# Parameter loads and later weight pieces issued once x's first half is turned: two waits moved in the SP queue of a three-layer transformer kernel

## The chip, the cores and the metric

One core of a Trainium2 chip runs the whole program. Its engines are TensorE (PE; PEld is its weight load), VectorE (DVE), ScalarE (ACT), GpSimd (POOL) and SyncE (SP), which here only issues DMA transfers. The metric is the device time of one execution in microseconds (us), and the kernel before is told by the median of three runs.

## The reference, cut to what matters

```
x = first_block(x, ...)          # mixer with GLA and dilated attention, then 32 experts, top 2
x = second_block(x, ...)         # two layers:
for i in range(2):
    hn = rms_norm(h, g_mix[i]);  z = hn @ w_in[i]            # in_0, in_1
    h = h + concat(gating(z_a), rwkv7(z_b), nsa(z_c)) @ w_out[i]
    hn = rms_norm(h, g_ffn[i])
    f = swiglu(hn, ...) if i == 0 else moe_swiglu(hn, ...)   # dense, then 8 experts, top 2
    h = h + f
    gate = sigmoid(rms_norm(h, g_ple[i]) @ ple_gate_w[i])    # ple_g
    h = h + (p[i] @ ple_proj_w[i]) * gate                    # ple_p
return rms_norm(h, g_final)
```

256 tokens, 1024 features, everything in float32. Inside `rwkv7` each row of z is mixed with the row before it, `z = z_b + (z_prev - z_b) * mu`.

## The kernel before, in words

**Order of the work.** Each engine has one hand-written list of instructions, and semaphores tie them. The stages are: the first block's mixer, the first expert stage (`moe1`), `in_0`; then in one stage the mixer of layer 0, its output projection, the dense layer, `ple_p0`, `ple_g0` and `in_1`; then the mixer of layer 1, the second expert stage (`moe2`), and last `ple_p1`, `ple_g1` and the final norm.

**The stream of weights.** All weights come in pieces of 1 MB (128 partitions by 2048 floats, 1.05 MB), in the order of their use, into a ring of nine slots (`RAW = 9`). The SP queue issues them: `stream` waits, for piece n, until TensorE has used piece n - 9, which had the same slot (`sp.wait_ge(used, p.n - RAW + 1)`), and then issues the transfer. SP works strictly in order, so whatever it waits for holds everything behind.

**Splitting.** A product runs as three matmuls on an upper and a lower part. ScalarE casts a landed piece into its upper part (L586, `split_high`), VectorE subtracts that to get the lower part in place (L590, `split_low`), TensorE then uses the piece (L566 to L568, 24 matmuls). `split_until` sends both ahead of TensorE by a few pieces, at places written out by hand in each engine's list; a piece that hasn't landed holds ScalarE there, with all that stands behind.

**Turning x.** Before a product with x, TensorE transposes x in two halves of four chunks each (`turn_half`, L667, eight transposes a half). Every chunk counts up the semaphore `xT_psum`. ScalarE evacuates the upper part with the norm's gain (L689), VectorE the lower part (L693). `XT_AT[name]` is the count before the transposes of one product, so `XT_AT[name] + KC // 2`, that is plus 4, is its first half turned.

**The expert stages' end.** TensorE scatters the last results (L2109, L2110) and VectorE adds them to x (L2294). Then each engine tests whether an expert has more tokens than fit (`overfull`) and, where none has, jumps over the code of an overflow pass (`stage_moe_rest`). Behind the jump stand, for ScalarE and VectorE, the splits of the next one or two pieces, and for TensorE the transposes of x.

**The SP queue around `in_0`.** `in_0` has twelve pieces. SP issued 0 to 5, waited until the last expert piece was used, and issued the 20 parameter loads of layer 0 (`load_layer`, L816: rows, small matrices and two transposed position tables), then pieces 6 to 9. Behind them stand four copies within SBUF that shift z by one row (`shift_sp`, L2511 to L2515, once ScalarE has evacuated the second job), which VectorE's mix (L2523 to L2525) waits for together with the parameter loads. ScalarE's two sigmoids (L2600, L2601) follow on that mix, and TensorE's small products of L2553 and L2559 on those.

**The SP queue around `ple_g`.** After the last piece of the feed-forward part come one piece of `ple_p` and four of `ple_g` (two blocks of 512 columns, each in two halves of the contraction), then, in layer 0, the pieces of `in_1`. In `ple_part(0)` ScalarE casts `ple_g0`'s piece 1 between the upper parts of x's two halves, with two result copies (L3503) behind it; pieces 2 and 3 follow after the squares of the norm (L710). In `ple_part(1)` all transposes come first, and pieces 1 to 3 are cast from the norm on.

Of the kernel before, what the change touches and what calls it, by code (L numbers as in the profile page):

```python
# [31 lines left out]
KC = D // P  # L32
# [85 lines left out]
def emit(nc, d, out):  # L118
    ctx = ExitStack()
    with ctx:  # L120
# [5 lines left out]
        def sem(name):  # L126
            return ctx.enter_context(nc.semaphore(name))
# [79 lines left out]
        upper, split, used = sem("upper"), sem("split"), sem("used")  # L207
# [49 lines left out]
        def sig(name):  # L257

            name = step_place[name][0] if name in step_place else name
            if name not in sems:  # L260
                sems[name] = sem(name)
            return sems[name]

        def ended(name, k=1, layer=0, per_layer=0):

            if name in step_place:
                _, before, total = step_place[name]
                return sig(name), layer * total + before + k
            return sig(name), layer * per_layer + k
# [4 lines left out]
        jobs_of, pieces_of = {}, {}  # L274
# [23 lines left out]
        def project(name, weight, kc, width, engines, group, first=0, striped=False, blocks=None, banks=(0, 1, 2, 3), k_first=False):  # L298
# [46 lines left out]
            for k, part in enumerate(parts):  # L345
                n = sum(m for _, m in part)
                places = [sum(m for _, m in part[:i]) for i in range(len(part))]
                chunks = kc if kc * n <= PIECE else kc // 2
                for c in range(0, kc, chunks):
                    p = new_piece([(0, chunks * n, rows[:, c:c + chunks, c0:c0 + m], n, at) for (c0, m), at in zip(part, places)], group)  # L350
                    p.c0, p.chunks, p.width, p.last = c, chunks, n, c + chunks == kc
                    pieces_of[name].append(p)
                    if c == 0:
                        jobs(p, k if blocks else part[0][0], n, 0)
                    else:
                        p.jobs = pieces_of[name][-2].jobs
                    if p.last:
                        done(p)
# [89 lines left out]
        moe1 = plan_moe("moe1", d["w_gate"][0], d["w_up"][0], d["w_down"][0], N_GROUPS, PER_GROUP, DE1, d["norm2_g"])  # L448
# [39 lines left out]
        def stream(sp, pieces):  # L488
            for p in pieces:
                if p.n >= RAW:  # L490
                    sp.wait_ge(used, p.n - RAW + 1)
                for dst, src in p.copies:
                    sp.dma_start(dst, src).then_inc(piece_ready[p.slot], 16)
# [34 lines left out]
        def stream_moe(sp, f):  # L528
            lot = [p for st in f.plan for p in st.up] + [p for st in f.plan for p in st.down]
            stream(sp, sorted(lot, key=lambda p: p.n))  # L530
            sp.wait_ge(sig("counted"), f.number)
            with overfull(sp, f):
                sp.wait_ge(used, f.until)
                m2 = Pass()
                stream_bucket(sp, f, m2, 0)
                with sp.Fori(1, f.buckets) as g:
                    stream_bucket(sp, f, m2, g)
                sp.wait_ge(*m2.at("used", f.buckets * f.steps))
            sp.end_ifs()
            if f is moe1:  # L540
                sp.sem_inc(sig("rest_streamed"), 1)
# [186 lines left out]
        XT_AT = {name: KC * k for k, name in enumerate(XT_ORDER)}  # L728
# [85 lines left out]
        def load_layer(eng, l):  # L814
            for dst, src in layer_loads(l):
                eng.dma_start(dst, src).then_inc(sig("layer_params"), 16)  # L816
# [1686 lines left out]
        def shift_sp(sp, l, part):  # L2503

            cols = (slice(512, 1024), slice(0, 512))[part]
            done = sig(f"rw_prev{part}")
            sp.wait_ge(evac_act, max(j.evac for j in jobs_of[f"in_{l}"][2 * part:2 * part + 2]))
            zb = z[:, :, ZB0:ZC0][:, :, cols]
            prev = w_prev[:, :, cols]
            even = P - 16  # L2510
            sp.dma_start(prev[1:even + 1], zb[0:even]).then_inc(done, 16)  # L2511
            for t in range(NT):
                sp.dma_start(prev[even + 1:P, t, :].rearrange("p (a n) -> p a n", a=16),
                             zb[even:P - 1, t, :].rearrange("p (a n) -> p a n", a=16)).then_inc(done, 16)
            sp.dma_start(prev[0:1, 1, :].rearrange("p (a n) -> p a n", a=16),  # L2515
                         zb[P - 1:P, 0, :].rearrange("p (a n) -> p a n", a=16)).then_inc(done, 16)
# [1133 lines left out]
        @block.sync  # L3650
        def _(sp):

            sp.dma_start(x[:], d["x"][0].rearrange("(t p) n -> p t n", p=P)).then_inc(sig("x_ready"), 16)
            sp.dma_start(g1T[:], d["norm1_g"][0].rearrange("(p c) -> p c", c=KC)).then_inc(sig("x_ready"), 16)
            stream(sp, pieces_of["in_ab"][0:3])
            for dst, src in G_LOADS:
                sp.dma_start(dst, src).then_inc(sig("g_params"), 16)
            stream(sp, pieces_of["in_ab"][3:7])
            for dst, src in P1_LOADS:
                sp.dma_start(dst, src).then_inc(sig("params"), 16)  # L3660
            stream(sp, pieces_of["in_ab"][7:])
            for name in ("gates", "y_gla", "y_att", "out_1"):
                stream(sp, pieces_of[name])
            stream_moe(sp, moe1)
            for l in range(LAYERS):
                pieces = pieces_of[f"in_{l}"]
                if l == 0:
                    stream(sp, pieces[0:6])
                    sp.wait_ge(used, moe1.until)
                    load_layer(sp, 0)  # L3670
                    stream(sp, pieces[6:10])
                else:
                    stream(sp, pieces[0:10])
                shift_sp(sp, l, 0)
                stream(sp, pieces[10:])
                shift_sp(sp, l, 1)
                stream(sp, cmp_pieces[l])
                stream(sp, pieces_of[f"out_{l}_2"])
                if l == 0:
                    sp.wait_ge(*ended("nsa_cmp", 1))  # L3680
                    load_layer(sp, 1)
                    stream(sp, sorted([p for up in ffn.up for p in up] + ffn.down, key=lambda p: p.n))
                else:
                    stream_moe(sp, moe2)
                stream(sp, pieces_of[f"ple_p{l}"])
                stream(sp, pieces_of[f"ple_g{l}"])

        @block.tensor
        def _(pe):
# [41 lines left out]
```

## Time and profile before

| | |
|---|---|
| median of 3 runs | 2472.41 us (2471.65 to 2475.49) |
| profiled execution | 2472.59 us, span 2470.8 us, mean granted TensorE clock 0.971 |
| PE busy | 2319.1 us (94%) |
| DVE busy | 1842.4 us (75%) |
| ACT busy | 1467.2 us (59%) |
| DMA | 617.64 MB, 250 GB/s over the span |

All times in the rows are from the start of the span. The profiled execution's own time is 1.8 us longer than its span. In the timeline a row is one instruction, or several alike in a row (x4), with the time from the start of the first to the end of the last; in square brackets stands how long the engine was idle ahead of it and what ended that. "issue" there means that nothing which the profile shows was waited for. SPq rows are DMA issues by the SP queue. In the rows of DMA queues q1 carries the SP queue's transfers, q8 and q14 carry instructions to the engines.

### The profile page before, as it was taken

How to read it: one execution, taken by the hardware profiler on the slowest of the kernel's cores; microseconds unless marked ns; L12 is line 12 of the kernel's file. 1: busy time of each engine (PE TensorE's matmuls, PEld its weight loads, DVE VectorE, ACT ScalarE, POOL GpSimd, SP SyncE). 2: the span in 40 equal slices, each digit the busy share in tenths (PEclk: the TensorE clock that was granted, in tenths of full speed). 3: DMA queues.
4: the chain of work that ended last, by engine and by line, in shares of the span. 5: the costliest groups of instructions: out<-in, count | busy, mean ns of one | idle time of the engine just before them, and what ended most of it. 6: DMA issues, size and time to landing. Idle time of an engine off the chain costs nothing.

```text
span 2470.8 us, 30555 instructions
## 1 busy us (share of the span) xinstructions
PE 2319.1 (94%) x12418; PEld 1891.6 (77%) x12418; DVE 1842.4 (75%) x1894; ACT 1467.2 (59%) x1400; POOL 49.6 (2%) x47
## 2 busy tenths in 40 slices
PE   7999987999999997988999998879999999999996
PEld 6878766888888885776788777668888888888885
DVE  5885658888898985776554577578888978888884
ACT  5354536776777774534443553466776767767764
POOL 0000000000000000020000002000000000000000
PEclk9999998999999998999999999989999999999999
DMA  9444445999999997406464551249999989999990
GB/s 231 128 124 136 153 145 186 363 367 358 366 359 367 357 368 231 138 3 196 138 203 171 166 163 50 81 177 363 356 366 357 358 300 349 358 368 355 366 344 34
DMA packets 281227, 617.64 MB, mean 250 GB/s; under 512 B 31848, under 2 KB 130408, under 8 KB 243696
## 3 DMA queue, kind: packets, MB, share of 16 engines
q1 hardware_dynamic: 279664, 611.33, 71.4%
q10 hardware_dynamic: 1408, 4.19, 0.5%
q8 instruction: 103, 1.69, 0.3%
q14 instruction: 52, 0.43, 0.1%
HBM read 612.34 MB, written 1.05 MB: 248 GB/s over the span
## 4 chain that ended last, share of the span: by engine, by line
PE 86%; DVE 7%; ACT 4%; issue 2%; POOL 0%; DMA 0%; DVEq 0%; ACTq 0%; SPq 0%
PE ps L566 25%; PE ps L567 25%; PE ps L568 25%; DVE ring_parts L590 2%; PE ps L2745 2%; PE ps L2098 1%; ACT high_parts L586 1%; PE ps L3023 1%; PE ps L667 1%; DVE arena L3280 0%; DVE arena L1325 0%; PE ps L3036 0%; PE ps L2068 0%; PE ps L2109 0%; PE ps L2110 0%
## 5 line engine op out<-in xcount | busy, mean ns | idle before, releaser
L590 DVE TENSOR_TENSOR ring_parts<-ring,high_parts 128x2048 fp32r<-128x2048 f32 (+1 forms) x574 | 1283.4, 2276 | 181.6 <-ACT high_parts L586 170.0
L586 ACT CAST high_parts<-ring 128x2048 fp32r<-128x2048 f32 (+1 forms) x574 | 1079.5, 1897 | 203.9 <-PE ps L568 190.6
L568 PE MATMUL ps<-high_parts,arena_parts 128*128 128x512 f32 (+2 forms) x1560 | 620.2, 398 | 0.0
L566 PE MATMUL ps<-high_parts,hT_parts 128*128 128x512 f32 (+2 forms) x1120 | 456.4, 408 | 30.5 <-DVE ring_parts L590 12.6
L567 PE MATMUL ps<-ring_parts,hT_parts 128*128 128x512 f32 (+2 forms) x1120 | 445.3, 398 | 0.0
L566 PE MATMUL ps<-high_parts 128*128 128x512 f32 x912 | 365.2, 400 | 0.0
L567 PE MATMUL ps<-ring_parts,high_parts 128*128 128x512 f32 x912 | 359.3, 394 | 0.0
L568 PE MATMUL ps<-high_parts 128*128 128x512 f32 x912 | 356.5, 391 | 0.0
L568 PEld LDWEIGHTS ps<-high_parts,arena_parts 128*128 128x128 f32 x1560 | 299.5, 192 | 68.9
L566 PE MATMUL ps<-high_parts,arena_parts 128*128 128x512 f32 x744 | 293.8, 395 | 3.2 <-DVE arena_parts L2273 2.3
L567 PE MATMUL ps<-ring_parts,arena_parts 128*128 128x512 f32 x744 | 292.9, 394 | 0.0
L566 PEld LDWEIGHTS ps<-high_parts,hT_parts 128*128 128x128 f32 x1120 | 217.9, 195 | 85.5 <-issue 21.4
L567 PEld LDWEIGHTS ps<-ring_parts,hT_parts 128*128 128x128 f32 x1120 | 217.6, 194 | 47.3
L568 PEld LDWEIGHTS ps<-high_parts 128*128 128x128 f32 x912 | 171.4, 188 | 41.7
L566 PEld LDWEIGHTS ps<-high_parts 128*128 128x128 f32 x912 | 172.1, 189 | 37.8
L567 PEld LDWEIGHTS ps<-ring_parts,high_parts 128*128 128x128 f32 x912 | 171.0, 187 | 35.7
L566 PEld LDWEIGHTS ps<-high_parts,arena_parts 128*128 128x128 f32 x744 | 140.3, 189 | 36.3 <-DVE arena_parts L2273 2.7
L2288 DVE SCALAR_TENSOR_TENSOR arena<-ps,arena 128x512 f32<-128x512 f32 x80 | 57.9, 724 | 147.7 <-PE ps L568 132.4
L567 PEld LDWEIGHTS ps<-ring_parts,arena_parts 128*128 128x128 f32 x744 | 140.1, 188 | 32.2
L2202 ACT CAST arena_parts<-ps 128x512 fp32r<-128x512 f32 x80 | 45.4, 567 | 140.1 <-PE ps L2098 140.1
L568 PE MATMUL ps<-high_parts,hT_parts 128*128 128x512 f32 x304 | 120.0, 395 | 0.0
L2220 ACT ACTIVATE arena<-ps 128x512 f32<-128x512 f32 x80 | 46.2, 578 | 68.0 <-PE ps L568 68.0
(525 smaller groups left out, 1831.0 us busy)
## 6 DMA issues: line engine op xcount, KB each, us to landing
ring<-in_moe_w SPq DMA_DIRECT2D x248, 1024.0 KB, 5.4
ring<-in_w_gate SPq DMA_DIRECT2D x64, 1024.0 KB, 5.3
ring<-in_w_up SPq DMA_DIRECT2D x64, 1024.0 KB, 5.2
ring<-in_w_down SPq DMA_DIRECT2D x64, 1024.0 KB, 5.3
ring<-in_w_in SPq DMA_DIRECT2D x104, 256.0 KB, 4.5
ring<-in_ffn_w SPq DMA_DIRECT2D x44, 512.0 KB, 4.8
ring<-in_w_in SPq DMA_DIRECT2D x20, 1024.0 KB, 5.0
ring<-in_moe_w SPq DMA_DIRECT2D x32, 512.0 KB, 4.8
```

The costliest lines, as they stand in the source:

```text
L566: pe.matmul(dst, a_hi, b_hi, start=first, stop=False, skip_group_check=True)
L567: pe.matmul(dst, a_hi, b_lo, start=False, stop=False, skip_group_check=True)
L568: return pe.matmul(dst, a_lo, b_hi, start=False, stop=last, skip_group_check=True)
L586: act.copy(high_flat(p), raw_flat(p)).then_inc(upper, 1)
L590: dve.tensor_tensor(raw_flat(p, ring_parts_flat), raw_flat(p), f32(high_flat(p)), ALU.subtract).then_inc(split, 1)
L667: mm = pe.transpose(ps[:, banks[c % 4 // 2], (c % 2) * S + t * P:(c % 2) * S + (t + 1) * P], src[:, t, c * P:(c + 1) * P], ident[:])
L2098: mm = pe.transpose(ps[:, TURN, c * P:(c + 1) * P], m_hid[:, 0:st.n][:, c::nc_], ident[:])
L2202: act.copy(m_hidT[:, 0:st.n // P, :].rearrange("p c n -> p (c n)"), ps[:, TURN, 0:st.n])\
L2220: act.activation(m_sg[:, 0:st.n], ps[:, GATE, 0:st.n], ACT.Silu).then_inc(sig("moe_silu"), 1)
L2288: dve.scalar_tensor_tensor(out=m_hid[:, 0:st.n], in0=src, scalar=m_gate[:, q:q + 1], in1=m_sg[:, 0:st.n], op0=ALU.mult, op1=ALU.mult).then ...
L2745: mm = pe.matmul(ps[rows, bank, i * RC:(i + 1) * RC], a[rows, i, :], b[rows, i, :], start=True, stop=True)
L3023: mm = pe.matmul(ps[0:CG * NCMP, CHAIN, k * P:(k + 1) * P], n_blk[:, k, i, :], w[:, i, :], start=(i == 0), stop=(i == 15))
```

## The change

SP's list gets two new waits on `xT_psum` and loses one on `used`. In `in_0`, pieces 4 and 5, the parameter loads and everything behind them are issued once the first half of x is turned for `mix0`. In both layers, pieces 1 to 3 of `ple_g` and everything behind them are issued once the first half of x is turned for `ple0` or `ple1`.

```
             for l in range(LAYERS):
                 pieces = pieces_of[f"in_{l}"]
                 if l == 0:
-                    stream(sp, pieces[0:6])
-                    sp.wait_ge(used, moe1.until)
+                    stream(sp, pieces[0:4])
+                    sp.wait_ge(sig("xT_psum"), XT_AT["mix0"] + KC // 2)
+                    stream(sp, pieces[4:6])
                     load_layer(sp, 0)
                     stream(sp, pieces[6:10])
                 else:
...
                 stream(sp, pieces_of[f"ple_p{l}"])
-                stream(sp, pieces_of[f"ple_g{l}"])
+                stream(sp, pieces_of[f"ple_g{l}"][0:1])
+                sp.wait_ge(sig("xT_psum"), XT_AT[f"ple{l}"] + KC // 2)
+                stream(sp, pieces_of[f"ple_g{l}"][1:])
```

On the SP queue at the end of the first expert stage (`ring` is the ring of weight pieces, `in_w_in` the weights of `in_0`), before (-) and in the change (+):

```order
-L493 DMA ring<-in_w_in 128x4x512 [waits used] x6
-L816 DMA arena<-in_rw_mu 128x1024 [waits used]
+L493 DMA ring<-in_w_in 128x4x512 [waits used] x4
+L493 DMA ring<-in_w_in 128x4x512 [waits used,xT_psum]
+L493 DMA ring<-in_w_in 128x4x512 [waits used]
+L816 DMA arena<-in_rw_mu 128x1024
 L816 DMA arena<-in_rw_w_2 128x256
 L816 DMA arena<-in_rw_a_2 128x256
```

No transfer changes its place in the queue; the fifth piece gets the wait on `xT_psum`, and the first parameter load loses its own.

On the SP queue at the end of the dense layer, ahead of the pieces of `in_1`:

```order
 L493 DMA ring<-in_ple_proj_w 128x2x1024 [waits used]
-L493 DMA ring<-in_ple_gate_w 128x4x512 [waits used] x4
+L493 DMA ring<-in_ple_gate_w 128x4x512 [waits used]
+L493 DMA ring<-in_ple_gate_w 128x4x512 [waits used,xT_psum]
+L493 DMA ring<-in_ple_gate_w 128x4x512 [waits used] x2
 L493 DMA ring<-in_w_in 128x4x512 [waits used] x10
```

The second gate piece gets the wait, and the ten pieces of `in_1` stand behind it. The same happens at the end of the second expert stage, where nothing stands behind.

## Rows read from the trace of the kernel before

**Rows 1.** The page: the chain by engine, and one kind of DMA issue.

```profile
PE 86%; DVE 7%; ACT 4%; issue 2%; POOL 0%; DMA 0%; DVEq 0%; ACTq 0%; SPq 0%
...
ring<-in_w_in SPq DMA_DIRECT2D x20, 1024.0 KB, 5.0
```

**Rows 2.** Timeline, end of the first expert stage: start, duration, engine, what, idle before.

```profile
953.42 0.34 SPq L816 DMA_DIRECT2D arena<-in_rw_mu  x1
...
959.04 3.70 ACT L586 CAST high_parts<-ring 128x2048 fp32r<-128x2048 f32 x2 [4.61 <-issue]
...
967.17 1.97 PE L667 MATMUL ps<-ident,x 128*128 128x128 f32 x8 [8.47 <-issue]
968.01 2.29 DVE L590 TENSOR_TENSOR ring_parts<-ring,high_parts 128x2048 fp32r<-128x2048 f32 x1 [8.58 <-issue]
...
970.63 0.43 SPq L816 DMA_DIRECT2D arena<-in_nsa_vc_w  x1
...
971.97 0.76 PE L566 MATMUL ps<-high_parts,hT_parts 128*128 128x512 f32 x1 [2.83 <-issue]
```

**Rows 3.** DMA queues in two stretches, 964.2 to 964.4 and 2422.6 to 2422.8.

```profile
q8 instruction: 1, 0.02, 42.6%
...
q8 instruction: 2, 0.03, 118.6%
```

**Rows 4.** Windows: engines' busy time, then granted PE clock, DMA share, GB/s.

```profile
955.00:970.00 15.00, 4.92 (x16) 3.38 (x16) 5.35 (x6) 5.36 (x6) 0.00 (x0) 0.56 0.79 145
...
2417.00:2424.00 7.00, 2.31 (x8) 1.35 (x8) 4.24 (x6) 2.29 (x2) 0.00 (x0) 1.00 0.27 83
...
973.00:980.00 7.00, 7.00 (x28) 5.55 (x27) 1.19 (x4) 2.12 (x5) 0.00 (x0) 0.70 1.05 393
989.00:994.00 5.00, 5.00 (x23) 4.01 (x22) 2.38 (x2) 2.10 (x2) 0.00 (x0) 1.00 0.42 112
```

**Rows 5.** Timeline of the SP queue: pieces 0 to 5 and the first shift copy.

```profile
928.59 14.73 SPq L493 DMA_DIRECT2D ring<-in_w_in  x6
...
989.34 0.73 SPq L2511 DMA_DIRECT2D arena<-arena  x1
```

**Rows 6.** Timeline, end of the second expert stage and the cast of `ple_g1`'s piece 1.

```profile
2419.32 1.90 ACT L586 CAST high_parts<-ring 128x2048 fp32r<-128x2048 f32 x1 [1.92 <-issue]
...
2424.24 2.29 DVE L590 TENSOR_TENSOR ring_parts<-ring,high_parts 128x2048 fp32r<-128x2048 f32 x1 [2.77 <-issue]
...
2426.76 3.68 PE L667 MATMUL ps<-ident,x 128*128 128x128 f32 x16 [6.24 <-issue]
...
2428.86 3.43 DVE L693 SCALAR_TENSOR_TENSOR arena_parts<-ps,l_gT,hT_parts 128x256 fp32r<-128x256 f32 x8 [2.33 <-ACT hT_parts L689]
...
2439.21 1.89 ACT L586 CAST high_parts<-ring 128x2048 fp32r<-128x2048 f32 x1
```

**Rows 7.** Timeline of the SP queue: first and last of layer 1's 20 parameter loads.

```profile
1112.06 0.34 SPq L816 DMA_DIRECT2D arena<-in_rw_mu  x1
...
1127.03 0.43 SPq L816 DMA_DIRECT2D arena<-in_nsa_vc_w  x1
```

**Rows 8.** Timelines of DVE and PE in `in_0`: the mix, and TensorE's wait behind it.

```profile
998.42 0.69 DVE L2523 TENSOR_TENSOR arena<-arena 128x512 f32<-128x512 f32 x1
...
1008.19 0.48 PE L2559 MATMUL ps<-arena 64*128 64x256 f32 x1 [1.86 <-DVE arena L2651]
```

**Rows 9.** Timelines of PE and ACT in `ple_part(0)`.

```profile
1369.94 1.03 PE L667 MATMUL ps<-ident,x 128*128 128x128 f32 x8
...
1380.08 0.40 PE L566 MATMUL ps<-high_parts,hT_parts 128*128 128x512 f32 x1
...
1372.06 1.93 ACT L586 CAST high_parts<-ring 128x2048 fp32r<-128x2048 f32 x1
...
1374.80 1.62 ACT L689 ACTIVATE hT_parts<-ps,l_gT 128x256 fp32r<-128x256 f32 x4
...
1380.07 3.69 ACT L586 CAST high_parts<-ring 128x2048 fp32r<-128x2048 f32 x2
```

## The prediction

> **What bounds the kernel now.** I read the page first: TensorE carries 86% of the chain that ended last [rows 1]. So time counts only where it comes on TensorE's path, and I looked at the three places at which the change moves a wait of the SP queue: the ends of the two expert stages and the end of the dense layer. There I read the timeline, for the bracketed idle time ahead of a row.
>
> At the end of the first expert stage the first transpose of x starts at 967.17, behind 8.47 us of idle put down to "issue": TensorE had been done since 958.70, and VectorE, which stands 8.58 us itself, had added its last to x by 959.43 [rows 2]. ScalarE stands 4.61 us. All three have just jumped over the code of the overflow pass, and the instruction queue's rows show what TensorE waits for: a block of q8 lands at 964.2, 5.5 us after its last matmul and 2.9 us ahead of the restart [rows 3]. Meanwhile the 20 parameter loads pass, issued from 953.42 to 971.06 [rows 2], and the DMA engines are busy to 0.79 [rows 4]. Weight pieces 4 and 5 are not among them: the last of the six was issued by 943.3 [rows 5] and had landed when the loads began.
>
> The second expert stage ends in the same jump without such loads (share 0.27) [rows 4]. There ScalarE stands 1.92 us, VectorE 2.77, TensorE 6.24 [rows 6]; two q8 blocks land at 2422.6, 2.1 us after TensorE's last matmul ended at 2420.52 [rows 3]. By this pair I price the change.
>
> The Trainium skill ("Runtime: NRT & Kernel Launch", section "Instruction fetch mechanics") says that a taken branch to code outside the fetched pages stalls the engine until a DMA has brought the page; the trace agrees, with the q8 block 2.9 us ahead of the restart.
>
> **The change, part by part.** It adds no work; only SP's waits move. The wait that goes, on the last expert piece, is implied by the new one: nothing.
>
> *First expert stage, the gain.* The loads no longer pass during the jump. ScalarE resumes at 954.43 + 1.92 = 956.4 and VectorE at 959.43 + 2.77 = 962.2 [rows 2, 6]. TensorE: 958.70 + 2.1 to the landing + 2.9 or 4.1 (both stages' time from landing to restart) = 963.7 or 964.8. I take 963.7, the one measured at this very jump. If the landing takes no more than ScalarE's 1.92 us of standing, VectorE is the last, from 962.2. Today VectorE must first split piece 0 (968.01, 2.29 us), and the first product with x starts at 971.97, 4.8 us after the transposes [rows 2]. At the second stage the lower halves begin 2.1 us after the first transpose, and four take 1.7 us (eight 3.43) [rows 6]: with VectorE early, the product starts 3.9 us behind the transposes, at 967.6. **Gain there 4.4 us**, bounds 3.2 (restart 964.8) and 5.8 (VectorE's 962.2 + 2.29 + 1.7 = 966.2).
>
> *What is late next.* SP starts when four chunks are turned, 963.7 + 2.0 (eight transposes, 1.97) = 965.7, and not at 953.42. It issues pieces 4 and 5, the 20 loads, pieces 6 to 9, and then the four copies that shift z by a row. Two pieces: 0.9 us, at 0.43 an issue as its last load. The loads: 17.6 us here, 15.4 for layer 1 (1112.06 to 1127.46) [rows 7]; I take 16.5, between them. So pieces 6 to 9 start at 983.1. The first lands 5.0 us later [rows 1]; they are 1.05 MB each, at the 393 GB/s of 973 to 980 [rows 4] 2.67 us apart, so the last lands at 983.1 + 5.0 + 8.0 = 996.1. In the old order they were through long before the shift copies were issued at 989.34 [rows 5]. Now those, wanted at 985, stand behind them in SP's ring, and take 2.1 us of their own (0.42 of the 5 us from 989 to 994 [rows 4]): 998.2. VectorE's mix waits for them; it started at 998.42 right behind the split of piece 5 [rows 8], would be ready at 994.0 with the gain, and finds its input at 998.2. ScalarE's sigmoids, the casts behind them and VectorE's copies hang on it, and TensorE has no slack there, since it waits 1.86 us for those at 1008.19 [rows 8]: it gives the gain back. **Net -0.2 us**, bounds -4.4 (copies not held; -5.8 with the best jump) and +3 (a late restart with loads of 17.6 us). Piece 6 lands at 988 and is used after six pieces of 5.7 us, near 1002: nothing.
>
> *Dense layer's end (ple0).* No jump stands here, so there is nothing to gain. The gate weights lay in the ring long before. Now pieces 1 to 3 are issued when the transposes of 1369.94 are done, at 1371.0 [rows 9], and the first lands at 1376.0, 3.9 us after ScalarE began its cast (1372.06). ScalarE works in order, so two result copies and the second half of x (1374.80) wait too. New: cast to 1377.9, copies to 1378.8, second half to 1380.4; VectorE's subtraction 1378.0 to 1380.3, then its four lower halves to 1382.0. TensorE came to that piece at 1380.08 without waiting [rows 9], so it stands 1.9 us. From the second half of x to the next casts (1374.80 to 1380.07) ScalarE needs 5.3 us [rows 9]: casts from 1384.1, so piece 2 is cast by 1386.1 and subtracted by 1388.4. TensorE is ready at 1382.0 + 5.7 (1374.4 to 1380.08 is one piece) = 1387.7: another 0.8. The other pieces have landed by then. The next turn of x follows from these gates, so all of it stays. **Cost 2.7 us**, bounds 1.5 and 4 (a landing 1.2 us earlier or later).
>
> *Second expert stage (ple1).* The gate pieces had landed before the jump (share 0.27, most of it a gain vector's), so nothing is gained. Now they are issued at 2426.76 + 2.0 = 2428.8, land at 2433.8, 2436.5 and 2439.2, and the first is cast at 2439.21 [rows 6], the others more than 3 us later. Cost 0; the cover of 5.4 us would end with a landing over 10 us.
>
> **Sum:** -0.2 + 2.7 + 0 = +2.5 us. The profiled execution took 2472.59 around its span of 2470.8, 0.18 over the median of 2472.41: so 2475.1 against it, **2474.9** on the median.
>
> **Rivals.** (A) *The fetch doesn't depend on the loads.* TensorE restarts at 967.17 as before, SP starts at 969.1, the shift lands at 1001.6, and the mix with all behind it is 3.2 us late; with ple0 +5.9: 2478.3. From a restart later than 963.9 on, the first stage loses. For it: TensorE stood 6.24 us with hardly a load about. Against: all three engines stood longer under the loads, and q8 landed 3.4 us later.
 The landing at 964.2 speaks against it.
> (B) *The copies aren't held*, because the loads are issued faster or the ring lets them by: 4.4 stays, less 2.7: 2470.7. For it: the mix had to wait for nothing before.
> (C) *B, and ple0 loses nothing*, TensorE having enough ahead: -4.4 to -5.8, 2468.0 to 2466.6.
> That the change doesn't do what it says is excluded by the order: the waits stand where the diff puts them.
>
> **Chances.** Forecast 0.52 (2472.5 to 2477.5), A 0.23, B 0.17, C 0.08. The range takes in B, and A with 2 us on top: 2469.5 to 2480.5; C and a double loss stay out. A measurement can tell about 0.2%, 4.9 us, from no change. Slower by more: most of A and a tenth of the forecast, 0.25. Faster by more: most of C, 0.07. Within: 0.68.
>
> **What would show it.** Right: first transpose near 963.7 behind 5 us of "issue"; the loads' first row behind it; VectorE's mix idle for about 4 us on the shift copies and starting at its old time; TensorE idle for 2 and 1 us in ple0 on VectorE's splits; ple1 as it was. Wrong: "issue" still at 8 us (A); the mix near 994 (B); no new idle in ple0 (C).

## The result and the profile after

The change is slower: 2483.66 us (median of 6 runs, 2480.49 to 2488.56) against 2472.68 (6 runs, 2470.17 to 2475.49), a ratio of 1.0043 with a 95% interval of 1.0033 to 1.0053. Of the 11.0 us the forecast had 2.5, and the result lies outside its range. The profiled execution took 2483.69 us around a span of 2481.9, so 11.1 more span than before; what follows is counted in that span.

First the page after, the chain by engine and the landing of the 1 MB weight pieces.

```profile
PE 85%; DVE 7%; ACT 3%; issue 2%; SPq 1%; DMA 1%; POOL 0%; DVEq 0%; ACTq 0%
...
ring<-in_w_in SPq DMA_DIRECT2D x20, 1024.0 KB, 9.1
```

Against [rows 1] SP's queue and DMA have each come into the chain with a percent, and the same pieces land after 9.1 us instead of 5.0. The kernel now waits for transfers that were hidden.

The end of the first expert stage, timeline after, as [rows 2] show it before (start, duration, engine, what, idle before).

```profile
954.23 1.01 ACT L2209 CAST arena_parts<-ps 128x1024 fp32r<-128x1024 f32 x1 [6.63 <-PE ps L568]
...
957.47 3.70 ACT L586 CAST high_parts<-ring 128x2048 fp32r<-128x2048 f32 x2 [2.22 <-issue]
...
962.75 1.97 PE L667 MATMUL ps<-ident,x 128*128 128x128 f32 x8 [3.27 <-issue]
963.31 2.29 DVE L590 TENSOR_TENSOR ring_parts<-ring,high_parts 128x2048 fp32r<-128x2048 f32 x1 [3.11 <-issue]
...
967.28 0.76 PE L566 MATMUL ps<-high_parts,hT_parts 128*128 128x512 f32 x1 [2.56 <-issue]
```

The cast at L2209 is the last work that the change can't touch; it starts at 954.23, before it was 953.42, so 0.8 us of every later difference is between the two executions and not the change's. The idle under "issue" fell from 8.47 to 3.27 us on TensorE, from 8.58 to 3.11 on VectorE, from 4.61 to 2.22 on ScalarE, and the first product starts at 967.28 instead of 971.97: with the 0.8 us, a gain of 5.5 us.

Then the SP queue, timeline after (start, time to issue, queue, what).

```profile
964.75 0.92 SPq L493 DMA_DIRECT2D ring<-in_w_in  x2
965.71 0.50 SPq L816 DMA_DIRECT2D arena<-in_rw_mu  x1
...
985.38 0.43 SPq L816 DMA_DIRECT2D arena<-in_nsa_vc_w  x1
985.85 2.25 SPq L493 DMA_DIRECT2D ring<-in_w_in  x4
988.14 2.92 SPq L2511 DMA_DIRECT2D arena<-arena  x1
991.10 2.81 SPq L2513 DMA_DIRECT2D arena<-arena  x2
```

The 20 loads take from 965.71 to 985.81, 20.1 us; the four pieces and the shift copies follow. The next rows are issues between 985 and 996 with their median time to landing, after.

```profile
ring<-in_w_in SPq DMA_DIRECT2D x4, 1024.0 KB, 10.1
...
arena<-arena SPq DMA_DIRECT2D x1, 448.0 KB, 12.9
arena<-arena SPq DMA_DIRECT2D x2, 30.0 KB, 9.4
...
arena<-arena SPq DMA_DIRECT2D x1, 2.0 KB, 11.1
```

Before, the copies in the same stretch:

```profile
arena<-arena SPq DMA_DIRECT2D x1, 448.0 KB, 3.5
arena<-arena SPq DMA_DIRECT2D x2, 30.0 KB, 2.7
arena<-arena SPq DMA_DIRECT2D x1, 2.0 KB, 3.7
```

What waits for them, and TensorE behind it, after:

```profile
1005.17 0.69 DVE L2523 TENSOR_TENSOR arena<-arena 128x512 f32<-128x512 f32 x1 [11.92 <-DMA arena<-arena]
...
1009.61 1.11 PE L2553 MATMUL ps<-ident,arena 128*128 128x128 f32 x4 [12.29 <-ACT arena L2601]
```

The mix stands 11.92 us and starts 6.75 us later than in [rows 8], TensorE's L2553 comes 6.74 later and has 12.29 us of idle where it had 0.28 (it started at 1002.87 before). With the 0.8 us taken off, the stage has lost 5.9 us, although its first product came 5.5 us early.

The end of the dense layer (`ple_part(0)`), timeline after, and a window in it (busy time of PE, PEld, DVE, ACT, POOL, then granted clock, DMA share, GB/s).

```profile
1377.55 1.03 PE L667 MATMUL ps<-ident,x 128*128 128x128 f32 x8
...
1378.62 1.47 SPq L493 DMA_DIRECT2D ring<-in_ple_gate_w  x3
...
1383.89 1.91 ACT L586 CAST high_parts<-ring 128x2048 fp32r<-128x2048 f32 x1 [4.08 <-DMA ring<-in_ple_gate_w]
...
1386.65 1.58 ACT L689 ACTIVATE hT_parts<-ps,l_gT 128x256 fp32r<-128x256 f32 x4
1389.84 0.47 PE L566 MATMUL ps<-high_parts,hT_parts 128*128 128x512 f32 x1 [1.98 <-DVE arena_parts L693]
```

```profile
1390.00:1394.00 4.00, 4.00 (x12) 3.15 (x12) 0.55 (x3) 3.97 (x6) 0.00 (x0) 0.63 1.05 387
```

ScalarE waits 4.08 us for the gate piece, TensorE 1.98 behind VectorE. Right behind that idle the granted clock is 0.63 of full speed: for most of the stretch TensorE is on the lower of its two levels (1.2 and 2.4 GHz), where a matmul takes 0.63 us instead of 0.39; before the change the stretch 1378 to 1392 had 1.00:

```profile
1378.00:1392.00 14.00, 14.00 (x65) 11.34 (x64) 7.42 (x8) 8.47 (x10) 0.00 (x0) 1.00 0.47 153
```

From this turn of x to the next it takes 25.14 us (1377.55 to 1402.69) instead of 21.35 (1369.94 to 1391.29): 3.8 us lost, about half by waiting, half by the clock.

The second expert stage lost nothing: its transposes stand 6.64 us under "issue" (6.24 in [rows 6]), the three gate pieces are issued at 2439.96 and land after 7.7, and the casts run on without a DMA in their brackets. TensorE's L667 there comes 11.2 us later than before, the end of the span 11.1. **The tally:** 0.8 between the executions, 6.8 by the turn of `ple0` (5.9 at the mix and some 0.9 on the way there), 3.8 in `ple0`, nothing after, together 11.4, against 11.1 at the end.

### The profile page after: what moved, and what is told of

The parts are those of the page before. It is cut to its first block, busy times and chain, and to the rows that moved or that the text cites. A ratio compares the mean times of both kernels' runs of the same rounds, so it can differ in the third digit from the quotient of the medians.

```text
span 2481.9 us, 30558 instructions
## 1 busy us (share of the span) xinstructions
PE 2324.9 (94%) x12418; PEld 1894.2 (76%) x12418; DVE 1842.4 (74%) x1894; ACT 1467.1 (59%) x1400; POOL 49.6 (2%) x47
## 4 chain that ended last, share of the span: by engine, by line
PE 85%; DVE 7%; ACT 3%; issue 2%; SPq 1%; DMA 1%; POOL 0%; DVEq 0%; ACTq 0%
PE ps L566 25%; PE ps L567 24%; PE ps L568 24%; DVE ring_parts L590 2%; PE ps L2745 2%; PE ps L2098 1%; ACT high_parts L586 1%; SPq L816 1%; PE ps L667 1%; PE ps L3023 1%; PE ps L3036 0%; DVE arena L3280 0%; PE ps L2109 0%; DMA arena<-arena 0%; PE ps L2110 0%
```

## The experiments

**The two parts alone.** `e1_in0_only` has the first hunk of the change on the kernel before, `e2_ple_only` the second. 

> The change's wait in in_0 alone, ple_g as in the kernel before. Additive theory: the loss is two separate ones, about 6 to 7 us here (jump shortened by 5 us, mix of in_0 about 6 us late) and about 3.7 us in ple0. Then this run is +6.5 us on the kernel before (5.5 to 8), and TensorE shows no new idle in ple_part(0). Rival: the loss in ple0 is only there because the stage before is late; then this run shows the whole +11 us.

> The two waits on ple_g alone, in_0 as in the kernel before. Additive theory: +3.7 us (2.7 to 4.5), all of it in ple_part(0), where TensorE waits about 2 us for piece 1 and 1 to 2 us for piece 2; nothing in ple_part(1). Rival: +0 to 1 us, the loss coming only together with the other wait; or a loss in ple_part(1) too, then over +5 us.

Measured: e1 2479.78 us (6 runs) against 2474.37 (21 runs), ratio 1.0026 [1.0012, 1.0039]; e2 2477.24 (11 runs) against the same 21, ratio 1.0011 [1.0001, 1.0021]. The timeline of e1:

```profile
963.85 1.44 PE L667 MATMUL ps<-ident,x 128*128 128x128 f32 x8 [2.88 <-issue]
...
1005.09 0.69 DVE L2523 TENSOR_TENSOR arena<-arena 128x512 f32<-128x512 f32 x1 [9.47 <-DMA arena<-arena]
```

and of e2:

```profile
1381.98 1.91 ACT L586 CAST high_parts<-ring 128x2048 fp32r<-128x2048 f32 x1 [3.89 <-DMA ring<-in_ple_gate_w]
...
1387.92 0.47 PE L566 MATMUL ps<-high_parts,hT_parts 128*128 128x512 f32 x1 [1.79 <-DVE arena_parts L693]
```

The parts add up within their intervals: 0.26% and 0.11%, together 0.37%, beside the change's 0.43%. e1 has its forecast (+6.4 us by the ratio), e2's +2.7 is at the lower end of its own. In e1 the turn-to-turn time of `ple0` is 21.34 us, in e2 24.91, so each loss has its own part of the diff as its cause. From L2209 to the first turn of `ple0` it takes 422.54 us in e1, 423.32 in the change, 416.52 before; e9, which leaves `in_0` as before, has 416.56, but e2, which does so too, 417.83: up to 1.3 us of this distance differ from one execution to the next.

**Are the copies what is late?** `e3_copies_first` keeps every wait of the first hunk, but issues the four shift copies ahead of pieces 6 to 9:

```diff
                     load_layer(sp, 0)
+                    shift_sp(sp, l, 0)
                     stream(sp, pieces[6:10])
```

(the call that stood behind is left for layer 1 alone). `e4_nine_ahead` asks whether the whole can be had by order: pieces 0 to 8 before the wait, loads and piece 9 behind it.

```diff
-                    stream(sp, pieces[0:6])
-                    sp.wait_ge(used, moe1.until)
+                    stream(sp, pieces[0:9])
+                    sp.wait_ge(sig("xT_psum"), XT_AT["mix0"] + KC // 2)
                     load_layer(sp, 0)
-                    stream(sp, pieces[6:10])
+                    stream(sp, pieces[9:10])
```

> As the change in in_0 (ple_g as before), but the four shift copies are issued ahead of pieces 6 to 9. Theory 'ring': the mix is late because its copies stand behind 4 MB of weights in the ring. Then they land by 992 to 994, the mix starts near 994, TensorE's idle ahead of L2553 falls from 12.3 us to under 2, and the shorter jump is kept: -3 to -5 us on the kernel before. Rival 'late loads': the parameter loads (20 us of issue, begun 12 us later) are themselves what comes too late, or the copies are slow on their own; then the mix still starts at 1000 or later and the run is +2 us or more. A late piece 6 (issued near 989, cast near 997) may cost up to 2 us in either.

> Pieces 0 to 8 of in_0 are issued as soon as their slots are free, only the parameter loads and piece 9 wait for the first half of x; ple_g as before. Theory 'ring': the copies have one piece and the loads' tail ahead, land by 994, mix near 994, and the jump stays short: -3 to -5 us. If weights in large packets slow the instruction fetch as the small loads do, piece 8 and the tail of 7 (issued near 950 and 953) lengthen the jump to about 5 us or more of idle, and the gain is halved (-2 us). Rival 'late loads': mix at 1000 or later, +2 us or more.

Measured, against the same 21 runs: e3 2467.96 us (9 runs), ratio 0.9977 [0.9967, 0.9987]; e4 2467.20 (6 runs), ratio 0.9968 [0.9956, 0.9980]. Both beat both kernels, e3 by 5.7 us and e4 by 7.9 on the kernel before, somewhat more than the 3 to 5 forecast. e3's timeline:

```profile
963.79 1.44 PE L667 MATMUL ps<-ident,x 128*128 128x128 f32 x8 [2.76 <-issue]
...
995.55 0.69 DVE L2523 TENSOR_TENSOR arena<-arena 128x512 f32<-128x512 f32 x1
```

e4's:

```profile
965.47 0.34 SPq L816 DMA_DIRECT2D arena<-in_rw_mu  x1
...
993.60 0.69 DVE L2523 TENSOR_TENSOR arena<-arena 128x512 f32<-128x512 f32 x1
```

With the copies ahead of the pieces, the mix has no wait and starts 9.5 us before e1's; all else is the same. That settles the mechanism: the copies stood in SP's ring behind four 1 MB pieces. In e3 they land after 3.5, 2.7 and 3.4 us. The distance from L2209 to the turn of `ple0` is 412.24 us in e3 and 410.45 in e4, 4.3 and 6.1 under before: this is what the shorter jump is worth when nothing gives it back, to 1.3 us. e4's loads take 16.4 us to issue (965.47 to 981.89), e3's 19.85: with pieces 4 and 5 in the ring ahead of the loads, the issue of the loads is 3.5 us longer. No run moved these two pieces alone, so that they are the cause is argued from the five cases: 15.4, 16.4 and 17.6 us without pieces ahead (layer 1, e4, before), 19.85 and 20.1 with them (e3, the change).

**What of the loads holds the fetch?** Two runs, one execution each, split the 20 loads: `e6_rows_in_jump` issues the first ten (a parameter row spread over 128 partitions, 1.6 MB in all) at the old place in the jump and the rest after the new wait, `e7_small_in_jump` the last ten (matrices and short rows, 0.6 MB).

```diff
                     sp.wait_ge(used, moe1.until)
-                    load_layer(sp, 0)
+                    load_layer(sp, 0, slice(0, 10))      # e7: slice(10, 20)
+                    sp.wait_ge(sig("xT_psum"), XT_AT["mix0"] + KC // 2)
+                    load_layer(sp, 0, slice(10, 20))     # e7: slice(0, 10)
                     stream(sp, pieces[6:10])
```

And `e5_weights_in_jump2` gives the second jump, which has hardly a transfer in it but the final norm's gain vector, the four gate pieces of `ple_g1` (4 MB in large packets):

```diff
+                if l:
+                    sp.wait_ge(used, moe2.until)
                 stream(sp, pieces_of[f"ple_g{l}"])
```

> The kernel before, but the four gate pieces of ple_g1 (4 MB in packets of 2 KB, no small ones) are issued once the last expert piece of the second stage is used, so that they pass during the second jump. Theory 'any traffic': the fetch waits behind whatever the DMA engines have taken; TensorE's idle ahead of its transposes rises from 6.2 us to 8 or more, and VectorE's from 2.8 to 5 or more. Rule 'in turn, packet by packet' or theory 'small packets only': they stay within 1 us of 6.2 and 2.8.

> The kernel before, but only the first 10 parameter loads (rows spread over 128 partitions, 1.6 MB) are issued at the last expert piece's use; the other 10 (matrices, position tables in single floats, 0.6 MB) and pieces 6 to 9 once x's first half is turned. If the spread rows slow the fetch, TensorE's idle stays at 7 to 8.5 us; if the small packets do, it falls to about 4.

> The other half: the 10 loads of matrices and position tables are issued at the last expert piece's use, the 10 spread rows after the turn. If the small packets slow the fetch, TensorE's idle stays at 7 us or more; if the spread rows do, it falls to about 4. If any traffic counts, both halves show 5 to 7 us.

Measured (one run each, before 2472.24; a single run's total says little here): e5 2473.11, e6 2472.86, e7 2467.97 us. e5's window over the jump, and its timeline:

```profile
2417.00:2425.00 8.00, 2.31 (x8) 1.34 (x8) 4.30 (x6) 2.52 (x3) 0.00 (x0) 0.98 0.96 351
```

```profile
2422.50 1.90 ACT L586 CAST high_parts<-ring 128x2048 fp32r<-128x2048 f32 x1 [4.88 <-issue]
...
2427.51 2.29 DVE L590 TENSOR_TENSOR ring_parts<-ring,high_parts 128x2048 fp32r<-128x2048 f32 x1 [5.82 <-issue]
2427.67 3.67 PE L667 MATMUL ps<-ident,x 128*128 128x128 f32 x16 [6.92 <-issue]
```

e6's timeline at the first jump:

```profile
968.38 1.97 PE L667 MATMUL ps<-ident,x 128*128 128x128 f32 x8 [8.75 <-issue]
```

and e7's:

```profile
961.73 1.17 PE L667 MATMUL ps<-ident,x 128*128 128x128 f32 x8 [2.94 <-issue]
```

With the DMA engines at 0.96 the second jump costs ScalarE 4.88 us instead of 1.92 and VectorE 5.82 instead of 2.77 [rows 6], and the last q8 block lands at 2424.8 instead of 2422.6. So it isn't the parameter loads as such: 4 MB of weights in large packets hold these two engines for about 3 us more as well. e4 has the same in the first jump: its pieces 7 and 8 pass there first (the last of the nine is issued by 955.0, the DMA share is 1.04 from 955 to 958), and ScalarE, the first to jump, stands 4.61 us as before, TensorE only 3.68. TensorE's forecast for e5, 8 us or more, was missed: it stands 6.92 us, 0.7 more than before, within the band that the expectation gave to the rival. It restarted 2.9 us behind the landing and not 4.1 [rows 3, 6]; what that means is taken up with the second jump below. Of the loads, the spread rows alone bring TensorE's whole stall back (8.75 us), the small ones none of it (2.94, against 2.76 to 3.68 in e1, e3 and e4, where no load is in the jump). The two differ in bytes and in kind, so which of these counts isn't told apart. e7 at 2467.97 also shows the mix unheld (993.59).

**The second jump's own stall.** [Rows 4] show a DMA share of 0.27 there, most of it one vector: the final gain, which ScalarE loads for all partitions. `e8_nine_gain_later` is e4 with that load issued behind the upper parts of x and the next cast in ScalarE's list instead of ahead of them; it goes out at 2424.96, when the jump is over.

```diff
-                    act.dma_start(o_gain, ...).then_inc(sig("final_gain"), 16)
                     evac_half(act, "act", name, gain, low_2, 0, BANKS[0])
                     evac_half(act, "act", name, gain, low_2, 1, BANKS[1])
                     split_until(act, "act", group, 2)
+                    act.dma_start(o_gain, ...).then_inc(sig("final_gain"), 16)
```

> Nine pieces of in_0 ahead of the wait, loads behind it (as e4), and ScalarE issues the final norm's gain vector (0.5 MB spread over 128 partitions) behind its upper halves of x instead of right after the second jump. If that load is what lengthens the second jump, TensorE's idle there falls from about 6 us to 3.5 or less, and the run is -7 to -10 us on the kernel before; if not, the idle stays and the run is -5 to -7 us as e4.

> The 10 loads of matrices and position tables at the last expert piece's use, the 10 spread rows and pieces 6 to 9 after the turn of x's first half (as e7), and the final norm's gain vector issued behind the upper halves of x (as e8); ple_g as before. Both jumps then run free of spread rows: TensorE idle about 3 and about 4 us where it was 8.5 and 6.2, mix not held. -7 us on the kernel before (-5 to -9). If only one of the two counts, -3 to -5.

(`e11_small_gain_later` is e7 with the same edit.) Measured: e8 2467.04 us (12 runs) against 2472.24 (17), ratio 0.9975 [0.9965, 0.9986]; e11 2467.09 (11 runs) against 2471.52 (21), ratio 0.9979 [0.9970, 0.9988]. e8's timeline:

```profile
2421.28 3.63 PE L667 MATMUL ps<-ident,x 128*128 128x128 f32 x16 [3.90 <-issue]
```

The stall fell from 6.24 us to 3.90 (4.03 in e11), VectorE's and ScalarE's stayed (2.83 and 1.92). By the totals (-6.2 and -5.2 us by the ratios) nothing was gained on e4: e8's forecast of -7 to -10 was missed, e11 lies in its range, and e4, e8 and e11, as e3, lie within their intervals of each other. Nor do the stalls show that the vector was the cause. With the vector at its old place TensorE's stall is 5.35 to 6.64 us in seven runs (before, the change, e1, e3, e4, e7, e9), but 4.44 in e10, 3.50 in e2 and 2.68 in e6, and there the vector passes in the jump as well (e6's timeline):

```profile
2427.29 3.13 PE L667 MATMUL ps<-ident,x 128*128 128x128 f32 x16 [2.68 <-issue]
```

What goes with the long kind is the instruction queue. Where two q8 blocks land within 0.4 us of each other (before, the change, e1, e3, e4, e7, e9), TensorE restarts 3.9 to 4.2 us behind them; where one lands (e2, e5, e6, e10), 2.4 to 2.9. e8 has one block and 2.5 us, but e11, without the vector as well, has two and 3.9. So some 1.7 of the 2.3 us by which e8 is better than the kernel before come with the number of blocks, and e11 shows that this isn't the vector's doing. From the first matmul of L2109 to the last block's landing it takes 3.7 us in e8 and 3.8 in e11, and 3.9 to 5.0 with the vector in place: by that the vector can have cost 0.1 to 1.3 us. Why there are now one and now two blocks stays open.

**Why does the last copy land so late?** `e10_copies_alone` is e1 with SP waiting for the copies before it issues pieces 10 and 11, so that nothing stands behind them:

```diff
                 shift_sp(sp, l, 0)
+                if l == 0:
+                    sp.wait_ge(sig("rw_prev0"), 64)
```

> The change's wait in in_0 alone (as e1), with one wait more: SP issues pieces 10 and 11 of in_0 only when the first four shift copies have landed. If the copies land late (19 us after piece 6's issue where 15 were worked out) because transfers issued behind them share the DMA engines, they land 2 to 4 us earlier, the mix starts 8 us instead of about 9.5 us after it could, and TensorE's idle ahead of L2553 falls from 9.8 to 6 to 8 us. If the ring moves them strictly in order, nothing changes (9.8 +- 0.5).

Measured, one run: 2473.95 us (before 2471.52, e1 2479.78 in its own runs). Its windows and timeline:

```profile
989.00:998.00 9.00, 9.00 (x40) 7.21 (x40) 3.62 (x2) 3.28 (x3) 0.00 (x0) 1.00 1.05 394
1000.00:1002.00 2.00, 0.00 (x0) 0.00 (x0) 0.00 (x0) 0.00 (x0) 0.00 (x0) 0.94 0.44 94
1002.00:1003.00 1.00, 0.00 (x0) 0.00 (x0) 0.00 (x0) 0.00 (x0) 0.00 (x0) 0.50 0.06 23
1002.00:1004.00 2.00, 0.00 (x0) 0.00 (x0) 0.20 (x1) 0.00 (x0) 0.00 (x0) 0.50 0.03 11
```

```profile
1003.79 0.69 DVE L2523 TENSOR_TENSOR arena<-arena 128x512 f32<-128x512 f32 x1 [8.39 <-DMA arena<-arena]
```

The wait is 8.39 us instead of 9.47: the pieces behind the copies cost 1.1 us of it. TensorE's idle ahead of L2553 is 8.76 us instead of 9.83, between the two forecasts (6 to 8 if the pieces behind share the engines, 9.8 if nothing changes): they do share them, and it is worth half of what was expected. The pieces ahead and the copies fill the engines until about 1001, as the forecast had it, but the last copy is signalled only at 1003.7. From 1002 to 1003 the share is 0.06 at 23 GB/s, with one packet every 0.08 us: that is one of the 16 engines at its part of the full 394 GB/s, still working its packets off while the others have none. So the tail of some 2 us is, for the most part, one engine that is behind. Why it is behind isn't shown.

**Is `ple0`'s loss the first late piece?** `e9_ple0_two_ahead` is e2 with two gate pieces ahead of the wait instead of one.

```diff
-                stream(sp, pieces_of[f"ple_g{l}"][0:1])
+                stream(sp, pieces_of[f"ple_g{l}"][0:2])
```

> in_0 as in the kernel before; in both ple stages gate pieces 0 and 1 go ahead of the wait, 2 and 3 behind it. If the loss in ple0 is piece 1 landing after ScalarE wants to cast it, it is gone: piece 2 lands near 1376 against a cast at 1380, TensorE has no new idle and the run is 0 +- 1 us on the kernel before. Rival: pieces 2 and 3 or in_1's behind them are late as well, then +1 to +3 us.

Measured: 2472.68 us (11 runs) against 2471.52 (21), ratio 1.0005 [0.9996, 1.0014], no difference that can be told. Turn to turn it takes 21.34 us again (1370.20 to 1391.54). The loss hangs on piece 1 alone; pieces 2 and 3 come in time.

## Why the prediction was wrong, step by step

**The jump: right, a little too small.** The stall does hang on the transfers in it, and rival A falls: the idle went from 8.47 to 3.27 us, and e6 brings it back with half of the loads. The forecast restart was 963.7 and is 961.95 with the 0.8 us taken off, 1.75 earlier. The term that was too large is the landing of the q8 block, taken from the second jump as 2.1 us behind TensorE's last matmul; in the change it lands at 960.0, 0.5 us behind the last one. The time from landing to restart, taken as 2.9, is 2.75. The pair that priced it wasn't alike: the second jump had a gain vector and two q8 blocks in it, and which of these delays the landing isn't told apart. The gain at the first product was 5.5 us and not 4.4, inside the bounds of 3.2 and 5.8. That q8 carries what TensorE waits for was read from its place in time alone; q14 blocks land in the jumps too, the last before a restart at 965.8 before and at 961.4 in the change, and no row ties a queue to an engine. As for the rule behind A: the Trainium skill ("DMA: Bandwidth & Descriptors", section "Queues, rings and completion order") speaks of packets of several descriptors, some 9 to 17, so that one packet's time would be "no microseconds" was the prediction's own step and not the page's.

**"What is late next": the step that failed.** Its mechanism stands: the copies are held behind pieces 6 to 9, and e3 shows it by moving them alone. Two of its terms were too small. The first is the issue of the loads, taken as 16.5 us from 17.6 and 15.4: it took 20.1, with pieces 4 and 5 now in the ring ahead of them; e4, without these, has 16.4, the forecast's value. Both rows that I took the price from were of an empty ring: [rows 5] have the first six pieces issued by 943.3, and ahead of layer 1's loads, from 1100 to 1112, the DMA share is 0.01. The second is the landing of the last copy, taken as 15.1 us (5.0 + 8.0 + 2.1) behind the first issue of piece 6: it came 19.2 us behind it (985.85 to 1005.1). In e10, with nothing behind the copies, it is 17.4 (986.35 to 1003.7): so 1.8 of the 4.1 us belong to the pieces 10 and 11, which share the engines (by e10's shorter wait it is 1.1), and some 2 to the tail, in which one DMA engine is still at work. SP started its issues a little earlier than forecast, 964.75 against 965.7. So the last copy is due at 998.2 - 1.0 + 3.6 + 4.1 = 1004.9, and landed at 1005.1. Net: -0.2 became +5.9 us, with the bound of +3 well short of it (its own terms, a restart 1.1 us later and loads 1.1 us longer, come to only +2).

**`ple0`: mechanism right, 2.7 became 3.8.** TensorE's first idle was put at 1.9 us and is 1.98. The second, put at 0.8, didn't come. In its place 1.8 us went to the granted clock (0.63 for the 4 us behind the idle), in the change and in e2 alike (0.61), and in e9, where there is no idle, it is gone. No term of the sum had a clock in it. The two hang together: VectorE had piece 2 subtracted at 1396.07, and at full clock TensorE would have come to it at 1389.84 + 5.7 = 1395.5 (an estimate) and waited 0.5 us; at the lower clock it came at 1397.06 and didn't wait. So the 2.7 was good for what it counted, and the clock added some 1.2.

**`ple1`: right, 0.** The gate pieces landed 7.7 us after their issue, and the forecast had allowed them 10.

**Rivals B and C** fell with the copies. Their time, 2466.6 to 2470.7, is what e3, e4, e7, e8 and e11 measured, with orders that hold the copies no longer. The range missed by 3.2 us: it took the bounds of single terms, 3 us on the first stage, and had no price for what a full ring does to each step that is queued in it.

## What to carry to other kernels

When a wait in front of a queue is moved, work out the queue's contents at its new place: an issue that took 16 us from an empty ring took 20 with 2 MB ahead of it, and copies that took 3 us to land took 9 to 13 behind 4 MB. Put the small transfer that a consumer wants soonest ahead of the large ones; here that single swap (e3) turned a loss of 0.26% into a gain of 0.23%. And where a code jump must be crossed, keep transfers out of it, and issue the bulk before it and not behind it (e4).

## What the runs showed of the hardware that was not expected

- At the jump over the overflow code TensorE stood 2.8 to 3.7 us at the first stage without the spread rows under way, and 8.5 to 9.2 with them (before, e2, e5, e6, e9). 4 MB of weights at the second stage did much the same to ScalarE (1.92 to 4.88) and VectorE (2.77 to 5.82), so small packets aren't needed for it.
- From the landing of the last q8 block to TensorE's restart it took 2.4 to 3.0 us where a single block landed, at either stage, and 3.9 to 4.2 where two landed within 0.4 us of each other (eight runs, second stage). Why is open.
- Small copies in a ring behind 4 MB of weights landed after 9 to 13 us instead of 3 to 4, and the last of them was held for some 2 us by what reads as one DMA engine that was behind the other 15 (e10).
- 1.8 to 2.0 us of idle in `ple0` were followed by 4 us at a granted clock of 0.61 to 0.63, which cost about as much as the idle itself. The kernel before has the same a little later, in `in_1`: 2.54 us of idle ahead of 1406.97, then a clock of 0.57 from 1407 to 1411.
